# The scan of an RWKV-7 layer in blocks: the factor kept once and turned on VectorE, the next pair's work spread group by group between the steps

## The reference, cut to what matters

```
def rwkv7_scan(r, w, k, v, a_vec, b_vec):
    def step(S, inp):
        r_t, w_t, k_t, v_t, a_t, b_t = inp
        sa = jnp.einsum('bhvk,bhk->bhv', S, a_t)
        S = S * w_t[:, :, None, :] + sa[..., None] * b_t[:, :, None, :] + v_t[..., None] * k_t[:, :, None, :]
        y = jnp.einsum('bhvk,bhk->bhv', S, r_t)
        return S, y
    S0 = jnp.zeros((B, H, N, N), jnp.float32)
    _, y = lax.scan(step, S0, xs)
    return jnp.moveaxis(y, 0, 1)
```

## Time and profile before

| what | value |
|---|---|
| median of 3 runs | 3930.97 us (3930.24 to 3931.32) |
| the profiled execution | 3932.74 us, its span 3931.0 us |
| PE, DVE, ACT, POOL busy, share of the span | 92%, 64%, 39%, 30% |
| the scan, from its first PE product to its last | about 1630.6 to 2059.4 us |

### The profile page before, as it was taken

The page is one execution under the profiler, slowest core; times in us unless marked ns, Lnnn a source line. Parts: engine busy times, 40 slices in busy tenths (PEclk is TensorE's granted clock), DMA queues, the critical chain, the costliest instruction groups (busy, mean ns, idle before and its releaser), DMA issues. The chain is left out here.

```text
span 3931.0 us, 62700 instructions
## 1 busy us (share of the span) xinstructions
PE 3622.7 (92%) x27516; PEld 2952.7 (75%) x27516; DVE 2515.6 (64%) x2223; ACT 1537.4 (39%) x1634; POOL 1171.2 (30%) x537
## 2 busy tenths in 40 slices
PE   8999999999989998877787999999998999997897
PEld 6778788878767776677774788887886888875775
DVE  5554767687756857644446566678767888817532
ACT  5563433344534338644435433334443222113412
POOL 1125454555412211233322455545530000000211
PEclk9999999999999999999998999999998999998998
DMA  2112233254122335612203032344312222231422
GB/s 96 49 38 62 77 106 105 97 177 161 62 81 70 120 120 176 210 63 68 68 26 134 27 110 94 113 169 145 105 57 99 76 75 81 81 125 40 152 95 102
DMA packets 187055, 384.08 MB, mean 98 GB/s; under 512 B 15952, under 2 KB 84816, under 8 KB 181008
## 3 DMA queue, kind: packets, MB, share of 16 engines
q1 hardware_dynamic: 149216, 307.72, 23.9%
q10 hardware_dynamic: 37568, 72.36, 5.0%
HBM read 273.60 MB, written 105.91 MB: 97 GB/s over the span
## 5 line engine op out<-in xcount | busy, mean ns | idle before, releaser
L3764 POOL MEMSET ssm_toep<- 128x4096 f32 x1 | 3.5, 3512 | 544.6 <-POOLq L3463 544.6
L3350 DVE SCALAR_TENSOR_TENSOR H<-hy_cu,par,H 128x1024 f32<-128x1024 f32 x120 | 153.5, 1279 | 0.0
L269 POOL TENSOR_TENSOR wlo1C<-fast_raw,whi1C 128x1024 fp32r<-128x1024 f32 (+1 forms) x40 | 112.5, 2812 | 112.0 <-ACT whi1C L259 112.0
L269 POOL TENSOR_TENSOR wlo0B<-fast_raw,whi0B 128x1024 fp32r<-128x1024 f32 (+1 forms) x40 | 113.0, 2824 | 107.6 <-ACT whi0B L259 107.6
L3350 DVE SCALAR_TENSOR_TENSOR hy_odd<-hy_cu,par,hy_odd 128x1024 f32<-128x1024 f32 x112 | 143.2, 1279 | 0.0
L269 POOL TENSOR_TENSOR wlo1A<-fast_raw,whi1A 128x1024 fp32r<-128x1024 f32 (+1 forms) x40 | 111.4, 2786 | 104.0 <-ACT whi1A L259 104.0
L269 POOL TENSOR_TENSOR wlo1B<-fast_raw,whi1B 128x1024 fp32r<-128x1024 f32 (+1 forms) x39 | 107.7, 2761 | 113.9 <-ACT whi1B L259 113.8
L1007 DVE TENSOR_TENSOR fast_xl<-fast_xr,fast_xh 128x2048 fp32r<-128x2048 f32 (+1 forms) x42 | 127.7, 3062 | 21.1 <-ACT fast_xh L848 21.1
L269 POOL TENSOR_TENSOR wlo0A<-fast_raw,whi0A 128x1024 fp32r<-128x1024 f32 (+1 forms) x40 | 109.1, 2727 | 104.8 <-ACT whi0A L259 104.8
L269 POOL TENSOR_TENSOR wlo0C<-fast_raw,whi0C 128x1024 fp32r<-128x1024 f32 (+1 forms) x39 | 108.1, 2771 | 104.4 <-ACT whi0C L259 104.4
L942 DVE TENSOR_TENSOR fast_g<-fast_g,flow_rms 128x1024 f32<-128x1024 f32 x44 | 128.1, 2912 | 1.5
(11 more groups left out here) (1446 smaller groups left out, 12079.0 us busy)
## 6 DMA issues: line engine op xcount, KB each, us to landing
fast_raw<-ffn_in_dram SPq DMA_DIRECT2D x88, 512.0 KB, 4.0
fast_xr<-ffn_x SPq DMA_DIRECT2D x28, 1024.0 KB, 6.0
sc_ops<-rw_arbkv SPq DMA_DIRECT2D x15, 1280.0 KB, 6.2
fast_raw<-ffn_out_dram SPq DMA_DIRECT2D x32, 512.0 KB, 3.8
wraw1A<-hybrid_in_dram SPq DMA_DIRECT2D x24, 512.0 KB, 3.5
wraw1B<-hybrid_in_dram SPq DMA_DIRECT2D x24, 512.0 KB, 3.6
ffn_x<-fast_g ACTq DMA_DIRECT2D x22, 512.0 KB, 3.3
ffn_x<-fast_e ACTq DMA_DIRECT2D x22, 512.0 KB, 2.8
```

Of the source, the lines that this page charges most:

```text
L269: eng.tensor_tensor(self.slot(wlo, n), self.raw[n], self.slot(whi, n).bitcast(fp32), ALU.subtract)\
L3350: op = dve.scalar_tensor_tensor(out=acc, in0=c[:, j:j + T], scalar=w, in1=acc, op0=ALU.mult, op1=ALU.add)
```

## The change

Three things are changed in `rwkv_scan`, with the order on every engine.

1. X is kept once, in `XX[.., 0, ..]`. `raw` makes one product instead of two for each m and e, `x_tile` two for each m instead of four; `raw_out`, `eye` and `x_out` are one instruction each instead of two. The transpose, which `w_tile` needs, is made by DVE: `turn_over` issues two transposes of 64 x 512 (32 x 32 blocks, which is enough up to the level of 32), after `eye` and after each level but the last. X's update goes to a bank of its own beside that of W.
2. `w_beside` puts the X products of one chunk between the W products of the other, block by block, where each was a step of its own.
3. The work of the neighbouring pairs is spread: one `in_time` or one half of `score` between two such steps, the raw products last. `state` is split into S, yu (`out_of_scores`) and ys (`out_of_state`).

```diff
-                                for e in range(2):
-                                    r = half(e if z == 0 else 1 - e)
-                                    mm = pe.matmul(eight[place(("raw", n, e))][r, m, :], x[half(e), m, w, :], x[half(e), m, y, :],
-                                                   start=True, stop=True)
+                            for e in range(2):
+                                mm = pe.matmul(eight[place(("raw", n))][half(e), m, :], x[half(e), m, BT, :], x[half(e), m, AT, :],
+                                               start=True, stop=True)
...
+                    def x_tile(n, l, m):
+                        a = n % 2
+                        for e in range(2):
+                            mm = pe.matmul(eight[2 * a + 1][half(e), m, :], Wt[half(e), a, m, :], XX[half(e), n % 4, 0, m, :],
+                                           start=True, stop=True)
+                        return mm
...
+                    def w_beside(n, l, x=None, u=None):
+
+                        if x is not None:
+                            pe.wait_ge(*after("sc_W", order(*x) + 1))
                         w_ready(n, l)
+                        if u is not None:
+                            u_ready(u)
                         for m in range(DT):
                             w = w_tile(n, l, m)
                             if m == DT - 1:
                                 w.then_inc(*tick("pe_W"))
+                            if x is not None:
+                                last_x = x_tile(*x, m)
+                            if u is not None:
+                                last_u = u_tile(u, m)
...
-                    def x_step(n, l):
...
-                                if l < LEVELS - 1:
-                                    mm = pe.matmul(eight[2 * a + e][half(1 - e), m, :], x, w, start=True, stop=True)
...
+                        w_beside(a, 0, u=n0 if before else None)
+                        in_time(p, 1, 1)
+                        w_beside(b, 0, x=(a, 0))
+                        if before:
+                            state(n0)
+                            out_of_scores(n0)
+                        w_beside(a, 1, x=(b, 0))
+                        if before:
+                            out_of_state(n0)
+                            u_step(n0 + 1)
+                        w_beside(b, 1, x=(a, 1))
+                        if before:
+                            state(n0 + 1)
+                            out_of_scores(n0 + 1)
+                        w_beside(a, 2, x=(b, 1))
+                        if before:
+                            out_of_state(n0 + 1)
                         if ahead:
                             in_time(p + 1, 0, 0)
+                        w_beside(b, 2, x=(a, 2))
+                        if ahead:
+                            score(n1, (0,))
+                        w_beside(a, 3, x=(b, 2))
+                        if ahead:
                             in_time(p + 1, 0, 1)
+                        w_beside(b, 3, x=(a, 3))
                         if ahead:
+                            score(n1, (1,))
+                        w_beside(a, 4, x=(b, 3))
                         if ahead:
                             in_time(p + 1, 1, 0)
+                            raw(n1)
+                        w_beside(b, 4, x=(a, 4))
                         if ahead:
+                            score(n1 + 1, (0,))
+                        x_alone(b, 4)
+                        if ahead:
+                            score(n1 + 1, (1,))
+                            raw(n1 + 1)
+                        last(a)
+                        last(b)
...
+                    def turn_over(n, name):
                         for e in range(2):
+                            dve.transpose(XX[half(1 - e), n % 4, 1, :, :].rearrange("p m t -> p (m t)"),
+                                          XX[half(e), n % 4, 0, :, :].rearrange("p m t -> p (m t)")).then_inc(*tick(name))
```

More of the change, by code:

```diff
@@ L2469, in claim, with claim_score @@
                 incs.append(by)
-            def claim_score(n):
-                for h in range(2):
+            def claim_score(n, halves=(0, 1)):
+                for h in halves:
                     for e in range(2):
@@ L2569, in _, with score @@
                 def _(pe):
-                    def score(n):
+                    def score(n, halves=(0, 1)):
                         x = ops[:, :, :, (n % 2) * CHUNK:(n % 2 + 1) * CHUNK]
-                        for h in range(2):
+                        for h in halves:
                             if n < 2:
@@ new lines, in _ @@
+                    in_time(0, 0, 0)
+                    in_time(0, 0, 1)
+                    in_time(0, 1, 0)
+                    for p in range(PAIRS):
+                        a, b, n0, n1 = 2 * p, 2 * p + 1, 2 * p - 2, 2 * p + 2
+                        before, ahead = p > 0, p < PAIRS - 1
+                        w_beside(a, 0, u=n0 if before else None)
[15 more added lines that the diff above has]
+                            out_of_state(n0 + 1)
@@ L2847, in _ @@
+                    for n in (NC - 2, NC - 1):
+                        u_out(n)
+                        y_out(n)
                 @block.gpsimd
@@ L2862, in ready @@
                     def ready(n):
-                        for e in range(2):
-                            pl.wait_ge(*gone(("raw", n, e)))
+                        pl.wait_ge(*gone(("raw", n)))
                     pl.wait_ge(*after("sc_const", 64))
@@ L4025, in step @@
         return (i // (2 * s) == t // (2 * s)) & (i % (2 * s) < s) & (t % (2 * s) >= s)
-    own = np.arange(P) // CHUNK
-    first = [np.where((own == e)[:, None], step(i, t, 1), step(t, i, 1)) for e in range(2)]
     return {"scan_mask": np.stack([i < t, i <= t], 1).astype(np.float32),
             "scan_level": np.stack([step(i, t, s) for s in (2, 4, 8, 16, 32)], 1).astype(np.float32),
-            "scan_first": np.stack(first, 1).astype(np.float32)}
+            "scan_first": step(i, t, 1).astype(np.float32)}
 def laid_out(v):
```

305 lines of the change are left out of this document (150 added, 155 removed).

## The result

The changed kernel takes 3902.22 us (median of 4 runs, 3900.11 to 3902.99) against 3930.6 for the kernel before beside it (4 runs, 3922.69 to 3931.32): ratio 0.9928, 95% interval 0.9914 to 0.9942. That is 28.4 us less, where 53.7 were forecast. The sign was right and the time lies in the stated range of 3858 to 3908, but outside the forecast's own 3865 to 3893 (chance 0.66): it fell where the rival "the stalls on top" stood (3893 to 3915, 0.18). The size was about twice too large.

What follows compares the result with a forecast made beforehand. PE in the scan was taken as bound by instruction blocks of 3.88 us each. Savings of 5.0 us (start), 48 (six pairs) and 0.7 (last pair) made 53.7: 3877.3 us, forecast 3865 to 3893 (0.66), stated range 3858 to 3908.

Steps and rivals of the forecast that it cites:

- the stalls on top: Rival for the whole kernel: PE's stalls add to whatever PE does; 3893 to 3915 us, chance 0.18.
- block account: Scan, pair before: 13.1 instruction blocks of 3.88 us on PE, 50.8, plus 1.4 waiting for BK, make 52.2 us.
- the stalls stay with the products: Rival, scan pairs: stalls come on top of PE's work, by number of products; pair 47.8, 3899 us, chance 0.18.
- stretch B: Steps 6 to 10 of a pair: DVE's chain decides, four steps of 3.3 to 3.5 us, 13.6 us.
- C: From step 10 to the next pair's U: the chain decides, 10.1 us, over 2.5 blocks or 9.8.
- The slow case: Rival: DVE's transposes take 1.277 us each instead of 0.69; pair 51.9, 3940 us, chance 0.06.
- The allowance of 0.9 for block ends inside B and C: Per pair, for instruction blocks ending inside dense steps: an estimated 0.9 us, raising 43.3 to 44.2.
- stretch A: From a pair's U step to step 6: instruction blocks decide, 5.04 of them, 19.6 us, over a chain of 16.65.
- The step that failed: SP's load of the next pair's 1280 KB, 2.5 us into a pair and needed some 12 later: no cost.
- The last pair: Last pair of the scan: 19.1, four chain steps 13.5, then 5.3; 37.9 us for 38.6, 0.7 less.
- The start: First pair, to its `last(b)`: first X 2.4 us earlier, end at 1686.5 instead of 1691.53, 5.0 us less.
- steps 2 to 10: Steps of the first pair, walked by the chain of products, add and transposes: 27.2 us.

Runs made afterwards that it cites:

- e3: The kernel before without the partner products of X (1024 of the scan's 6912 products), output incomplete: 3888.66 us, against 3930.36 for the kernel before.
- e5: The changed kernel with the load of the next pair's operands in four pieces, each released by a step: 3886.41 us, against 3928.43 for the kernel before.
- e2: The changed kernel with the load of the next pair's operands cut to 64 KB, output incomplete: 3884.75 us, against 3930.36 for the kernel before.
- e8: The changed kernel with the raw products of chunk n1 + 1 ahead of its scores: 3904.45 us, against 3928.43 for the kernel before.
- e10: The changed kernel with e5's four-piece load and both raw products in the gaps of stretch B: 3877.78 us, against 3928.43 for the kernel before.
- e7: The changed kernel with seven groups of 16 idle products in the gaps of the first and last pair: 3890.26 us, against 3928.43 before.

## Why the prediction was right in kind and half in size

**The block account held in kind.** 1344 records a pair as counted, and in the DMA view of the six pairs 64 instruction packets for 8,064 records where it was 66 in five:

```profile
q8 instruction: 64, 1.05, 1.5%
```

e3 shows products costing more than their array time, though at 4.3 us for two blocks and not at 7.8. That the account of the pair before closed at 52.2 was luck in part: the 3.88 came from nine stretches of which none holds the late packet, and beside the load each pair before already had an interval of 5.5 us, 1.6 over the others, which the account had as 1.4 for BK. With the packets' own intervals the pair is 5.5 + 12.1 x 3.85 = 52.1. The rival "the stalls stay with the products" gave a pair of 47.8 and 3899 us, nearly what came, but for another reason: it has no transfer in it, and with the transfer cut up (e5) or away (e2) the pair went to 45.2 and 44.8. The rival's number was right by luck, its mechanism falls; and it was this rival's share of the stated range that held the time.

The Trainium skill ("Runtime: NRT & Kernel Launch", Instruction fetch mechanics) has block crossings "mostly hidden". With a block of 3.88 us where 2.2 to 3.4 are worked, and 6.07 beside a transfer, this case's traces disagree.

**The chain held in stretch B.** Four steps of 3.51 for 3.3 to 3.5: products 1.17, add 0.69, two transposes 1.44, and three hand-overs of 0.03 to 0.11 where two of 0.05 were put. C is 9.8 for 10.1, but by e8 the chain alone doesn't hold it. The transposes, which I had bounded by 0.485 and 1.277 and taken at 0.69, measure 706 ns; groups by line and form, 1600 to 2060 us:

```profile
L2942 DVE STREAM_TRANSPOSE sc_XX<-sc_XX 64x512 f32<-64x512 f32 x160 | 112.9, 706 | 17.3 <-POOL sc_XX L2882 12.4
L2954 DVE TENSOR_TENSOR sc_XX<-psA,sc_XX 128x512 f32<-128x512 f32 x40 | 27.7, 692 | 47.3 <-PE psA L2634 47.3
```

The slow case is out. The allowance of 0.9 for block ends inside B and C was not needed; it covered a quarter of what A lost.

**The step that failed:** "SP's load of the operands comes after `in_time(p, 1, 1)`, now 2.5 us into the pair, and its 1280 KB are needed some 12 us later: no cost." I asked when the data are needed and not what else uses the DMA engines, though the last sentence of the prediction named it. The fetch of instructions comes late beside both halves: a packet interval of 6.6 us where 3.88 was priced, PE short of instructions for 2.85 to 4.16 us once in each pair, and stretch A 3.7 us too long in the pair shown, against 2.4 (e5) and 2.8 (e2) a pair that come back when the load is cut up or away. That is 14 to 17 of the 25.5 us missing from the scan's 53.7. The rest of the pair's 3.4 is B's 0.4 and, argued and not shown, the end of U at a granted clock of 0.56; e5 and e2 have their slower pairs at 0.93 to 0.96, e10 and e7 show no such relation, so what that clock costs in a full pair stays open. In the trace of before the longest idle time of each pair stood at the load already, 2.4 to 3.4 us.

**The last pair, 2.4 us over its 37.9 (40.3 to `last(a)`),** was worked out at full clock. That DVE's chain leaves PE idle for two thirds of a step stood in my own numbers; that the clock then halves did not. e7 shows it.

**The start, 2.5 us for a forecast of 5.0.** The first X came 2.6 us earlier after the scan's first product, for a forecast of 2.4, and the end from step 10 to `last(b)` took 8.9 as walked. What failed are the steps 2 to 10: 29.8 us for 27.2. Two of them take 4.34 and 4.35 us at granted clocks of 0.50 and 0.60, the other six 3.5. The 2.2 us behind the last pair are no shown effect of the change: in the same work e5 takes 1884.0 us from there to the end, e7 1884.6, the kernel before 1886.1, the changed kernel 1888.3.

## What to carry to other kernels

When an engine runs dense streams of small products, count its instructions as bytes that must arrive: a term of the bound is the number of blocks times the time of a block, and a large transfer in that stretch can be on the path, however early its data come. Look for the longest idle time beside it in the trace that is there already, and try it in pieces, each released by a step of the work: in the two kernels here that brought 13.6 and 4.6 us. Where a change shortens work on TensorE and lengthens a chain on another engine, price the sparse stretches at the lower clock too. Before a difference of a few us is put down to a change, compare where the changed part begins in both traces: here 3.8 us lay ahead of it.

## What the runs showed of the hardware that was not expected

- An instruction packet can come late beside data: none in the 5.1 us from 1787.1 to 1792.2 with queue 1 at 89%, and PE idle for 2.85 us. The packet interval with the load was 6.6 us in the mean of six pairs, 5.1 at the longest with the same bytes in four gated pieces and 4.0 with hardly any.
- The granted clock went to 0.50 after two steps with PE busy for a third of them, and stayed through 5.4 us of dense work in 6.1; groups of 16 idle products between the steps kept it at 1.00.
- "issue" as the end of a wait covers the want of instructions and a wait for a semaphore of DVE alike; only the other engine's timeline tells them apart.
